# Channel sums in strips of 128 tokens, output token by token, and a split first weight chunk

## What is computed

```python
# first block
h = rms_norm(x, norm1_g);  p = h @ w_in                    # 1024 -> 3328
br_a = gmlp_spatial_gating(gelu(u), gelu(v));  br_b = s5_mixer(s_in)
x = x + (g_a * (br_a @ w_up_a) + g_b * (br_b @ w_up_b)) @ w_out
h2 = rms_norm(x, norm2_g)
x = x + expert_choice_ffn(h2)        # softmax router, 16 experts, top 64 tokens each, 1024 -> 2048 -> 1024
x = rms_norm(x, final_g)
# second block
u = rms_norm(x);  x_lru, g_lru, q, k, v, g_ret = split(u @ w_in_2)
y_lru = rms_norm(rg_lru(conv(x_lru)) * gelu(g_lru));  y_ret = head_norm(retention(q, k, v)) * silu(g_ret)
x = x + concat(y_lru, y_ret) @ w_out_2
u = rms_norm(x);  x = x + (gelu(a) * v) @ ffn_down, [a, v] = conv(u @ ffn_up)     # 1024 -> 2 x 3072 -> 1024
return rms_norm(x)                                             # (512, 1024)
```

## Time and profile before

| | |
|---|---|
| median of 3 runs | 1888.03 us |
| profiled execution, its own time | 1889.88 us |
| its span | 1888.1 us |
| TensorE matmul busy | 1737.5 us (92%), 8120 instructions |
| VectorE busy | 668.1 us (35%) |
| ScalarE busy | 443.6 us (23%) |
| HBM traffic | 487.49 MB read, 2.10 MB written |

### The profile page before, as it was taken

One profiled execution on the slowest core, in us unless ns is written; L12 is line 12 of the kernel. 1 busy time (PEld: TensorE's weight loads), 2 busy tenths in 40 slices (PEclk: granted clock), 3 DMA queues, 4 the chain that ended last, 5 costly groups with the idle time before them and its releaser, 6 DMA issues. The chain is left out here.

```text
span 1888.1 us, 19429 instructions
## 1 busy us (share of the span) xinstructions
PE 1737.5 (92%) x8120; PEld 1038.7 (55%) x8120; DVE 668.1 (35%) x903; ACT 443.6 (23%) x546; POOL 0.2 (0%) x4
## 2 busy tenths in 40 slices
PE   6999996999897997979979799799999999999997
PEld 5888874343342432324323243257767788888885
DVE  7886533101010010101101001057645475645654
ACT  4534322110010100101000010065333343423332
POOL 0000000000000000000000000000000000000000
PEclk9999997999999999999999999999999999999999
DMA  5235436999999999999999999950402223222311
GB/s 183 82 91 174 161 140 250 400 428 428 427 428 428 430 428 428 428 429 428 429 428 428 428 427 428 427 195 1 178 27 87 88 89 112 89 89 89 111 45 44
DMA packets 76389, 492.47 MB, mean 261 GB/s; under 512 B 7472, under 2 KB 12592, under 8 KB 51504
## 3 DMA queue, kind: packets, MB, share of 16 engines
q1 hardware_dynamic: 76336, 491.71, 64.5%
HBM read 487.49 MB, written 2.10 MB: 259 GB/s over the span
## 5 line engine op out<-in xcount | busy, mean ns | idle before, releaser
L1182 PE MATMUL ps<-xs,xe 128*64 128x512 f32 x2048 | 461.5, 598 | 66.6 <-DMA xs<-w_up 35.3
L1182 PEld LDWEIGHTS ps<-xs,xe 128*64 128x64 f32 x2048 | 141.7, 137 | 379.1 <-issue 264.6
L1194 PE MATMUL ps<-xs,hidT 128*64 128x512 f32 x1024 | 229.8, 596 | 13.9 <-DMA xs<-w_down 9.2
L412 DVE TENSOR_TENSOR lo<-raw,hi 128x2048 fp32r<-128x2048 f32 (+1 forms) x73 | 164.8, 2258 | 174.6 <-ACT hi L403 171.4
L1409 DVE TENSOR_TENSOR hid<-hid,ps 128x512 f32<-128x512 f32 x32 | 20.6, 684 | 524.1 <-PE ps L1182 524.1
L403 ACT ACTIVATE hi<-raw 128x2048 fp32r<-128x2048 f32 (+1 forms) x73 | 138.0, 1890 | 218.5 <-PE ps L466 98.5
L466 PE MATMUL ps<-xh,hi 128*128 128x512 f32 x416 | 165.2, 397 | 0.8 <-DVE ga L931 0.8
L466 PE MATMUL ps<-xl,hi 128*128 128x512 f32 x416 | 162.2, 390 | 0.0
L1194 PEld LDWEIGHTS ps<-xs,hidT 128*64 128x64 f32 x1024 | 73.9, 136 | 148.2 <-issue 127.1
L442 PE MATMUL ps<-xh,hi 128*128 128x512 f32 x384 | 150.2, 391 | 1.1 <-DVE xt L1915 0.9
L442 PE MATMUL ps<-xl,hi 128*128 128x512 f32 x384 | 149.4, 389 | 0.0
(11 more groups left out here) (415 smaller groups left out, 1782.4 us busy)
## 6 DMA issues: line engine op xcount, KB each, us to landing
xs<-w_up SPq DMA_DIRECT2D x64, 2048.0 KB, 32.8
xs<-w_gate SPq DMA_DIRECT2D x64, 2048.0 KB, 32.0
xs<-w_down SPq DMA_DIRECT2D x64, 2048.0 KB, 31.3
raw<-w_in SPq DMA_DIRECT2D x25, 1024.0 KB, 6.7
raw<-ffn_up_w SPq DMA_DIRECT2D x24, 1024.0 KB, 5.1
raw<-ffn_down_w SPq DMA_DIRECT2D x12, 1024.0 KB, 5.1
raw<-w_out SPq DMA_DIRECT2D x8, 1024.0 KB, 5.0
xin<-x_t SPq DMA_DIRECT2D x4, 512.0 KB, 8.0
```

The source lines that it names most:

```text
L412: dve.tensor_tensor(lo[slot][:, 0:size], raw[:, raw_slot(n), 0:size], hi[slot][:, 0:size].bitcast(F32), ALU.subtract).then_inc(sem("lo_don ...
L1182: mm = pe.matmul(ps[64 * half:64 * half + 64, bank + b, :], xe[:, k, CAP * u:CAP * (u + 1)], xs[n % NXS][:, f:f + 512], start=(k == 0), st ...
L1194: mm = pe.matmul(ps[64 * nn:64 * nn + 64, YB, :], hidT[:, 4 * (c % 2) + kk, CAP * half:CAP * (half + 1)], xs[n % NXS][:, kk * D + nn * 512 ...
```

## The change

The channel sums are made in four strips: strip t is 32 partitions of the result and holds the sums of tokens 128t to 128t+127 (32 equal rows). Root and reciprocal then act on 128 x 128. Four matmuls with a selecting matrix (`pick`) spread a strip back over all partitions where a row over 512 tokens is needed, and one transpose gives the factors with tokens on partitions. Routing gathers logits and the sum (as row 16, `hot`) in one bank. The head sums go to rows 0 to 3 of the strips. The reciprocal of the FFN norm and the order of its first chunks move. The output is transposed on TensorE and stored by token. Chunk 0 is re-laid by the host as (128, 8, 256) and loaded and split in two halves, the first ahead of x's tiles, the second between them; x tiles 4 to 7 are one load.

```diff
+        def strip_sums(pe, i, bank):
+            for k in range(KD):
+                pe.wait_ge(sem("nrm_sq"), NSQ[i] + k + 1)
+                for t in range(NT):
+                    mm = pe.matmul(strip(bank, t), ones[:, 0:32], squares(i)[0][:, k, t * P:(t + 1) * P],
+                                   start=(k == 0), stop=(k == KD - 1))
+        def strip(bank, t, c=0):
+            return ps[32 * t:32 * t + 32, bank, c:c + P]
+        def strip_spread(pe, r, bank, c):
+            for t in range(NT):
+                mm = pe.matmul(ps[:, bank + t, c:c + P], pick[32 * t:32 * t + 32], r[32 * t:32 * t + 32], ...)
+            a(rs[0], ps[:, bank, 0:P], ACT.Sqrt, scale=1.0 / D, bias=eps)      # strip_root
...
 # start, TensorE
-            pe.wait_ge(sem("hi_done"), 1); pe.wait_ge(sem("lo_done"), 1)
             for k in range(KD):
+                if k % 4 == 0:   # waits for the half of chunk 0: c0_hi and c0_lo, then hi_done and lo_done
...
-            norm_sums(pe, 0, QQ + 3)
+            strip_sums(pe, 0, QQ + 3)
+            def spread_first():
+                pe.wait_ge(sem("rb_done"), 1)
+                strip_spread(pe, rs[0], PP, SW)
+                pe.transpose(ps[:, PP, SW + P:SW + 2 * P], rs[0], ident).then_inc(sem("rt_ps"), 1)
             chunk_mms(pe, 1, QQ, 0, 4, xh, xl, True, closes=False,
-                      after={(0, 2): lambda: pe.wait_ge(sem("nrm_rms"), 1)})
+                      after={(0, 1): spread_first, (0, 2): lambda: pe.wait_ge(sem("nrm_rms"), 1)})
 # start, ScalarE: first half of hi; two Exp; xh 0, 1; second half of hi; xh 2, 3; two Sin; xh 4 to 7; squares
 # start, VectorE: first half of lo; xl 0, 1; second half of lo; xl 2, 3; the small S5 operations; xl 4 to 7
...
-            inputs(0); dve.wait_ge(sem("nrm_rms"), 1); L(dve.reciprocal(rb[:], rb[:]))
+            inputs(0); dve.wait_ge(sem("nrm_rms"), 1)
+            dve.reciprocal(rs[0], rs[0]).then_inc(sem("rb_done"), 1)
 # routing, logits(k)
-                mm = pe.matmul(ps[o, LB, :], wrg[:, k, :], xt[:, k, :], start=(k < 4), stop=(k >= 4))
-                mm = pe.matmul(ps[o, SB, :], ones[:, 0:32], sqx[:, k, :], start=(k < 4), stop=(k >= 4))
+                for t in range(NT):
+                    pe.matmul(strip(LB, t), wrg[:, k, :], xt[:, k, t * P:(t + 1) * P], ...)
+                pe.wait_ge(sem("nrm_sq"), KD + k + 1)
+                for t in range(NT):
+                    mm = pe.matmul(strip(LB, t), hot[:, 0:32], sqx[:, k, t * P:(t + 1) * P], ...)
-  # copy 128x512 (VectorE), copy 128x512 (ScalarE), 4 + 4 small matmuls
+            for bank in (SB, LB):                       # behind one 128x128 copy on VectorE
+                mm = pe.transpose(ps[:, bank, 0:P], part[:], ident)
 # second norm: 16 matmuls of 64 x 512 become 32 of 32 x 256; spread_two behind tile 1 of chunk N2+1
+                pe.wait_ge(sem("rms_step"), 1)
+                for q in range(4):
+                    pe.matmul(ps[:, QQ + q, 256:512], pick[32 * q:32 * q + 32], rr[32 * q:32 * q + 32], ...)
+                for b in range(2):
+                    mm = pe.transpose(ps[:, QQ + 1, b * P:(b + 1) * P], rr[:, b * P:(b + 1) * P], ident)
 # LRU and heads: 4 x 4 strip matmuls each, and
+            def spread_lru():
+                pe.wait_ge(sem("rb_done"), 2); pe.wait_ge(sem("hstd_done"), 1)
+                strip_spread(pe, rs[0], 0, 2 * P).then_inc(sem("rt_ps"), 1)
+            def spread_heads():                         # 16 matmuls 32 x 128, waits for rv_done and spr_out
-            chunk_mms(pe, N2 + 11, ..., after={(0, 0): head_vars, (0, 3): spread})
-            pe.wait_ge(sem("mix_lo"), 4)
+            chunk_mms(pe, N2 + 11, ..., after={(0, 0): head_vars, (0, 1): spread_lru, (0, 3): spread_heads})
-            chunk_mms(pe, N2 + 12, PP, 0, 4, mh, ml, closes=False)
+            chunk_mms(pe, N2 + 12, PP, 0, 4, mh, ml, closes=False, by_tile=("mix_lo", 1))
 # ScalarE makes hi of N2+12 ahead of take_o(3), VectorE its lo ahead of the reciprocals
 # FFN start
-            norm_sums(pe, 4, QQ + 3)
-            chunk_mms(pe, NFFN + 1, QQ, 0, 4, ...); chunk_mms(pe, NFFN + 2, PP, 4, 4, ...); chunk_mms(pe, NFFN + 3, QQ, 4, 4, ...)
+            strip_sums(pe, 4, QQ + 3)
+            chunk_mms(pe, NFFN + 1, PP, 4, 4, ..., after={1: spread_fourth})
+            pe.wait_ge(sem("spr_out"), 3)
+            for h in range(2):
+                chunk_mms(pe, NFFN + 2 + h, QQ, 4 * h, 4, ...)
 # end, TensorE: last chunk
-                                  after={2: first_sums})          # 4 norm sums
+                                  after={1: first_turned, 2: first_sums})
+            # first_turned: 16 transposes; first_sums: 4 one-column sums, turned(4), turned(5)
-            norm_sums(pe, 5, PP, range(4, KD))
+            turned(6); token_sums(1, 4); turned(7); token_sums(2, 7)
 # end, VectorE and ScalarE
-            norm_scale(dve, chains["dve"], 5, xt)                 # reciprocal 128x512, 8 scalings
+            # xg = xt * gain (8), sq2 summed over tiles (5 additions), reciprocal 128x4,
+            # 4 scalings on VectorE from PSUM, 4 on ScalarE in xo
-                d(out[:, k, :], xt[:, k, :])                       # 8 stores
+                d(out[t * P:(t + 1) * P, :], xo[:, t, :])          # 4 stores
```

More of the change, by code:

```diff
@@ L265, in build @@
         sqx = at("sqx", [P, KD, SEQ], F32, B + 57)
-        part = [at(f"part{j}", [P, SEQ], F32, B + 51 + 2 * j) for j in range(2)]
+        part = at("part", [P, P], F32, B + 51)
         cst2 = at("cst2", [P, NCONST - NSMALL], F32, B + 38)
@@ L477, in chunk_mms @@
                             mm = one(part, m, kk)
+                    if kk in after:
+                        after[kk]()
             elif each:
@@ L1502, in lru_sum @@
                     pe.wait_ge(sem("lsq_done"), m + 1)
-                    mm = pe.matmul(ps[:, 0, :], ones, xc[:, m, :], start=(m == 0), stop=(m == 3))
+                    for t in range(NT):
+                        mm = pe.matmul(strip(0, t), ones[:, 0:32], xc[:, m, t * P:(t + 1) * P], start=(m == 0), stop=(m == 3))
                 mm.then_inc(sem("lsum_ps"), 1)
@@ L1569, in second_pe, with turned, token_sums, first_turned @@
             part(NFFN + 28, None, (j, 0))
-            def first_sums():
-                pe.wait_ge(sem("x3_done"), KD + 4)
-                norm_sums(pe, 5, PP, range(4))
+            def turned(k):
+                pe.wait_ge(sem("xg_done"), k + 1)
+                for t in range(NT):
+                    mm = pe.transpose(ps[:, PP + k, t * P:(t + 1) * P], xg[:, k, t * P:(t + 1) * P], ident)
+                mm.then_inc(sem("xT_ps"), 1)
+            def token_sums(n, k):
+                for t in range(NT):
+                    mm = pe.matmul(ps[:, PP, t:t + 1], sq2[:, k, t * P:(t + 1) * P], ones[:, 0:1],
+                                   start=(n == 0 and t == 0), stop=(n == 2 and t == NT - 1))
+                return mm
+            def first_turned():
+                for k in range(4):
+                    turned(k)
+            def first_sums():
+                pe.wait_ge(sem("xo_done"), 1)
+                pe.wait_ge(sem("acc_done"), 1)
+                token_sums(0, 0)
+                turned(4)
+                turned(5)
             for jd in (j - 1, j):
@@ L1934, in second_dve @@
             new_rest(range(4, KD))
-            make_lo(dve, NFFN + 2)
-            dve.wait_ge(sem("nrm_rms"), 4)
-            L(dve.reciprocal(r4[:], r4[:]))
+            dve.wait_ge(sem("nrm_rms"), 3)
+            dve.reciprocal(rs[0], rs[0]).then_inc(sem("rb_done"), 1)
             for h in range(2):
@@ L1995, in second_dve, with gained, summed @@
             add(PP, 0, "x3_done", True)
+            def gained(k):
+                dve.wait_ge(sem("x3_done"), KD + k + 1)
+                ts(xg[:, k, :], xt[:, k, :], gains[:, 5, k:k + 1], None, ALU.mult).then_inc(sem("xg_done"), 1)
+            def summed(k0, k):
+                dve.wait_ge(sem("nrm_sq"), NSQ[5] + k + 1)
+                L(tt(sq2[:, k0, :], sq2[:, k0, :], sq2[:, k, :], ALU.add))
+            for k in range(4):
+                gained(k)
+            for k in range(1, 4):
+                summed(0, k)
+            dve.sem_inc(sem("acc_done"), 1)
             for m in range(4):
```

319 lines of the change are left out of this document (179 added, 140 removed).

## The result

| | before | after |
|---|---|---|
| median (runs) | 1888.18 us (4) | 1860.15 us (4) |
| lowest to highest | 1887.39 to 1890.01 | 1859.35 to 1860.67 |
| profiled execution (span) | 1889.88 (1888.1) | 1860.12 (1858.4) |

The ratio is 0.985, 95% interval [0.984, 0.986]: 28.0 us faster, and 1860.0 had been forecast. The sum came out; its terms did not all. There are two profiles of the kernel before (spans 1888.1 and 1886.4), and the table gives the lead of the kernel after against both. The lead is the start of a piece of work in the kernel before minus the start of the same work in the kernel after, in us, so a term of the forecast is the difference of two rows.

What follows compares the result with a forecast made beforehand. Outside the experts TensorE's own instructions set the time; in the experts it waits for weight DMAs. Gains 4.1 + 4.4 + 3.6 + 10.1 + 4.8 + 1.0 = 28.0 give a median of 1860.0 us, range 1854 to 1869.5.

Steps and rivals of the forecast that it cites:

- Start: Start up to chunk 2: split chunk 0 and strips gain, a new wait for VectorE takes part; 4.1 us gained.
- Routing: Logits and sums before the top-64 search: cheaper logits 2.6, shorter chain behind the last chunk 1.8; 4.4 us gained.
- Rival (b): Experts: what is gained ahead of them vanishes behind DMA; 1868.5 us, chance 7%.
- Second norm: Second norm's sums: 7.1 us become 3.5, spread and transposes add 1.0, one-column matmuls (0.8) go; 3.6 us gained.
- LRU and head sums: LRU stage up to `mh`: 2.7 earlier, the 4.45 wait for `ml` and the slow clock (3.0) go; 10.1 us gained.
- Rival (c): LRU stage or `spread_two`: a chain cut too close, wait of 2 to 3 us and clock fall; 1865, chance 17%.
- FFN start: FFN norm's sums: 6.87 us become 1.75, spread costs 0.3; 4.8 us gained.
- End: Last output group to span end: TensorE transposes put it 2.7 us later, stores start earlier; 1.0 us gained.
- rival (a): All strip sums: strips go one after the other, so the kernel gets slower; 1893 us, chance 3%.
- Rival (d): Start: the clock does not fall or returns early, and other stages do a little better; 1857 us, chance 10%.

Runs made afterwards that it cites:

- the one with the filler: Changed kernel with 42 transposes of a constant block on TensorE ahead of its wait for the first reciprocal; 1860.65 us, ratio 0.985.

## Why the prediction was right, and where it was not

- **Start, 4.1 forecast, 3.1 and 2.3 found.** The mechanism was as forecast: an idle that VectorE's reciprocal ends, and the lower clock behind it. The sizes: the reciprocal ended at 34.9 instead of 34.0, since x 2 and 3 landed half a microsecond later and xl 7 ended at 19.25 instead of 18.5; the idle was 5.8 instead of 5.2; the lower clock cost 2.1, forecast 2.0. The 0.8 between 3.1 and 2.3 is luck of the two executions of before: their first 26 and 18 matmuls ran at 0.21 us instead of 0.12, and eight times 0.09 is 0.7. What I did not do is to set the forecast's own numbers against the start without the split: TensorE at 15.3, strips to 31, no idle, chunk 2 at about 42.6, which beats the 43.9 that I forecast with it. So the term counted the split as a gain where it was none: the measured gain is from the strips, and the split took 2.6 of it.
- **Routing, 4.4 forecast, 4.4 found** (7.54 - 3.12 and 6.71 - 2.32). Against the first profile 1.2 more appear behind the Exp, which the second shows to be the first one's clock. No run tests this term by itself.
- **Experts.** Rival (b), nothing arrives behind DMA, is refuted: from the Exp to the last scatter it is 945.3 and 944.3 us before, 945.1 and 945.3 after, although everything ahead had moved by 7 us. From the end of the top-64 search to the last scatter the lead fell by 0.7 (6.7 to 6.0, second profile) or 1.0 (first), no more.
- **Second norm, 3.6 forecast, 3.3 found.** The spreads are 0.71 + 0.44 instead of 1.0. Against both profiles of before 1.6 more come ahead of it, from the clock near 1236, which is full there in nine of the twelve later traces.
- **LRU and head sums, 10.1 forecast, 8.9 found** (21.5 - 12.6). The wait of 4.45 went whole. The clock gave 2.7 instead of 3.0. TensorE's own work between the LRU sum and `mh` gave 1.8 instead of 2.7: the LRU sum had taken 3.04 us, not 3.4, and takes 1.0 now, and the spreads are 0.50 and 1.17, where I had allowed 0.2 more than before. Rival (c) did not come: the covers of 0.9 and 0.1 us held. Moving hi and lo, which I counted as part of the chain, did nothing; the narrow reciprocals and the tile-by-tile wait for `ml` did it.
- **FFN start, 4.8 forecast, 4.2 found.** Strips 1.96 instead of 1.75, spread 0.50 instead of 0.3.
- **End, 1.0 forecast, 3.9 found.** This step failed: "16 transposes (0.88 per four)". The row 289.03 holds eight transposes, not four; I had taken two records for each, as the other float32 matmuls leave. At 0.11 instead of 0.22, 24 transposes are 2.6 us cheaper, nearly the whole difference. In the Trainium skill, Perfetto Trace Analysis, Transposes, a transpose skips the arithmetic of a matmul. The runs show the lower price, 0.11 us against 0.186 for a strip matmul of as many columns, not the reason for it.
- **Strips one after the other, rival (a)**: refuted where tried, 5.96 against 1.96. Rival (d) was wrong in the start, where the clock fell as forecast.

The median came out at 1860.15 against 1860.0 because the misses cancel: -1.4 (start), -0.3 (second norm), -1.2 (LRU and heads), -0.6 (FFN start), +2.9 (end), and some 0.9 given back in the experts against 1.6 from the clock near 1236. That was partly luck: by its terms the forecast was good to about 1 us each, with one error of 3.

## What to carry to other kernels

When TensorE's start is moved ahead, follow the other engine's order to the first thing that it hands back, and work out the old start with the same list: here the split of the first chunk cost 2.6 us until one reciprocal moved, and was worth 4.6 afterwards. A sum over partitions in strips of 32, one per quarter of the array and side by side, cost 1.96 us against 7.03 for the full-width sum, and the reciprocals that follow became narrow too (0.95 against 3.35), which took 4.9 us off the chain behind the longer wait. And count records before dividing by them.

## What was not expected of the hardware

- **One wait, two outcomes for the clock.** Behind the wait of 1.84 us near 1346 the granted clock was 1.00 in the kernel after, 0.66 in the one with the filler, 0.79 with hi and lo moved back, and the stretch from the LRU's gates to its sum took 103.56, 105.27 and 105.28 us. In the other eleven traces it took 103.4 to 103.6. The same happened near 290 and near 1230. So one profile carries 1 to 3 us that the kernel does not owe, as much as several edits here are worth, and single edits are better read from leads at milestones than from spans.
- **The rate in the first microseconds.** From 9.4 to 12 TensorE's matmuls follow each other at 0.21 us and then at 0.12, but the granted clock in the row for that stretch reads 1.00 (2.4 GHz):

```profile
9.40:12.00 2.60, 2.60 (x12) 2.60 (x13) 1.73 (x2) 1.67 (x2) 0.00 (x0) 1.00 1.00 411
```

  Thirteen real matmuls ran at the slow rate in this execution and 26 in the second one of the same kernel; 26 and 18 did in the two of the kernel before, 23 in the one with the early reciprocal, and none where twenty others stood ahead of them. So this too is chance of an execution, up to 1.2 us of TensorE's time. The rate has to be read from the distance of the matmuls.
